# One block's shift in the attention heads' order, z kept in another buffer, and two clears on GpSimd

## The reference, cut to what matters

```python
y_a = hyena_mixer(hy, ...) @ P['w_hy_out'][l]
...
kv = (ckv @ P['w_kvb'][l]).reshape(B, L, N_HEADS, NOPE_DIM + V_DIM)
...
s = jnp.einsum('bqhd,bkhd->bhqk', qi, k).astype(jnp.float32) * scale
p = jax.nn.softmax(s, axis=-1).astype(v.dtype)
return jnp.einsum('bhqk,bkhd->bqhd', p, v)
...
y = (g_a * y_a + g_b * y_b + g_c * y_c) @ P['w_out'][l]
```

## Time and profile before

| | us |
|---|---|
| median of 3 runs | 3128.07 |
| lowest, highest | 3124.54, 3131.0 |
| profiled execution, its own time | 3132.21 |
| its span, first to last instruction | 3130.4 |

### The profile page before, as it was taken

The page is one execution under the profiler, slowest core; times in us unless marked ns, Lnnn a source line. Parts: engine busy times, 40 slices in busy tenths (PEclk is TensorE's granted clock), DMA queues, the critical chain, the costliest instruction groups (busy, mean ns, idle before and its releaser), DMA issues.

```text
span 3130.4 us, 48654 instructions
## 1 busy us (share of the span) xinstructions
PE 3014.3 (96%) x19892; PEld 2936.5 (94%) x19892; DVE 2124.1 (68%) x3521; ACT 1140.6 (36%) x1820; POOL 83.7 (3%) x160
## 2 busy tenths in 40 slices
PE   7999999999999999999999999999999999999998
PEld 4899999998899899999999999999888999999998
DVE  7677666646655557988967897863665555775675
ACT  3422312322444434434433433442244443443432
POOL 0000000000000000000000000000000000000000
PEclk8999999999999999999999999999999999999999
DMA  8255553245122432343332433324611252222222
GB/s 305 90 215 218 222 192 141 109 165 223 71 72 92 186 110 80 102 153 131 129 108 75 142 122 135 129 104 168 245 71 71 75 208 83 75 88 81 95 68 75
DMA packets 89743, 408.90 MB, mean 131 GB/s; under 512 B 10049, under 2 KB 13569, under 8 KB 68914
## 3 DMA queue, kind: packets, MB, share of 16 engines
q1 hardware_dynamic: 60960, 287.86, 25.5%
q0 software_dynamic: 19296, 92.43, 8.1%
q10 hardware_dynamic: 9266, 25.50, 2.2%
HBM read 359.46 MB, written 46.30 MB: 130 GB/s over the span
## 4 chain that ended last, share of the span: by engine, by line
PE 77%; DVE 14%; ACT 5%; issue 3%; DMA 1%; ACTq 0%; DVEq 0%
PE tile_psum L743 20%; PE misc_psum L860 12%; PE tile_psum L750 11%; PE misc_psum L864 6%; PE tile_psum L1215 6%; PE tile_psum L704 3%; PE tile_psum L1219 3%; PE misc_psum L669 3%; PE tile_psum L669 2%; PE tile_psum L860 2%; PE tile_psum L709 2%; PE misc_psum L1153 1%; DVE h L2254 1%; PE tile_psum L1080 1%; DVE wlo L2083 1%
## 5 line engine op out<-in xcount | busy, mean ns | idle before, releaser
L743 PE MATMUL tile_psum<-n_hi,whi 128*128 128x320 f32 x1536 | 353.4, 311 | 4.0 <-issue 2.2
L743 PE MATMUL tile_psum<-n_lo,whi 128*128 128x320 f32 x1536 | 351.2, 309 | 0.0
L2083 DVE TENSOR_TENSOR wlo<-raw,whi 128x2048 fp32r<-128x2048 f32 (+4 forms) x130 | 250.5, 1929 | 120.0 <-ACT whi L1491 118.0
L743 PE MATMUL tile_psum<-x_hi,whi 128*128 128x320 f32 x1300 | 298.9, 310 | 19.2 <-DVE h L2254 19.2
L743 PE MATMUL tile_psum<-x_lo,whi 128*128 128x320 f32 x1300 | 297.1, 309 | 0.0
L743 PEld LDWEIGHTS tile_psum<-n_hi,whi 128*128 128x128 f32 x1536 | 257.6, 189 | 6.8 <-DVE n_lo L2174 4.2
L743 PEld LDWEIGHTS tile_psum<-n_lo,whi 128*128 128x128 f32 x1536 | 258.3, 189 | 0.0
L1491 ACT ACTIVATE whi<-raw 128x2048 fp32r<-128x2048 f32 (+4 forms) x130 | 208.9, 1616 | 129.8 <-DMA raw<-in_w_down 42.1
L1215 PE MATMUL tile_psum<-n_hi,whi 128*128 128x320 f32 x768 | 237.6, 320 | 11.7 <-ACT gate_out L1978 10.3
L2254 DVE SCALAR_TENSOR_TENSOR h<-tile_psum,ada_t,h 128x320 f32<-128x320 f32 (+2 forms) x408 | 154.1, 434 | 129.6 <-PE tile_psum L750 128.1
L750 PE MATMUL tile_psum<-n_hi,wlo 128*128 128x320 f32 x1536 | 241.4, 309 | 0.0
(11 more groups left out here) (384 smaller groups left out, 6439.0 us busy)
## 6 DMA issues: line engine op xcount, KB each, us to landing
raw<-in_w_up SPq DMA_DIRECT2D x72, 512.0 KB, 3.9
raw<-in_w_up SPq DMA_DIRECT2D x34, 1024.0 KB, 4.8
w_ada<-in_w_ada POOLq DMA_DIRECT2D x68, 512.0 KB, 4.1
w_ada<-in_w_ada SPq DMA_DIRECT2D x60, 512.0 KB, 6.1
raw<-in_w_gate SPq DMA_DIRECT2D x24, 1024.0 KB, 4.8
raw<-in_w_down SPq DMA_DIRECT2D x29, 768.0 KB, 4.4
whi<-table_keep SPq DMA_DIRECT2D x20, 1024.0 KB, 4.7
wlo<-table_keep SPq DMA_DIRECT2D x20, 1024.0 KB, 6.9
```

Source lines behind the costliest of these rows:

```text
L743: pe.matmul(tps[:, t.s, m, 0:TH], blk(p, m * n + k)[0], (hi, lo)[b][:, k, tok], start=k == 0 and b == 0, stop=False)
L2083: ins = dve.tensor_tensor(lo_at(r, n)[:, 0:w], raw_at(r, n)[:, 0:w], hi_at(h_, n)[:, 0:w].bitcast(F32), ALU.subtract)
```

## The change: what it does

The order: in each pair the queries of the second head (Q, a gate half, QS) move from before the pair's first score block to before its second one. In the first pair z's split becomes a step of its own (Z), after N0 and before V0. The result is `Q0 F K0 QS0 F S0 F Q1 F QS1 S1 F N0 Z0 V0 S2` and, for the later pairs, `Q2 F K2 QS2 S10 F N9 T8 F Q3 F QS3 S11 F N10 T9 F P1`. The number of steps of each kind stays the same.

The last product of the Hyena branch is written to `art[:, c]` (the buffer of the scaled low-rank rows) in place of `hyx`, and ScalarE waits for both halves once, ahead of the first Q. The two clears leave VectorE; GpSimd makes them in its queue, ahead of the third gate write, after a wait for z.

```diff
--- before.py
+++ after.py
@@ -257,11 +257,13 @@
     for n in range(5 * HEADS + 2):
         if n < 5 * HEADS:
             if n % 10 == 0:
-                for hd in (n // 5, n // 5 + 1):
-                    order += [("Q", hd), ("F", 0)] + [("K", hd)] * (hd % 2 == 0) + [("QS", hd)] + [("F", 0)] * (hd == 0)
+                order += [("Q", n // 5), ("F", 0), ("K", n // 5), ("QS", n // 5)] + [("F", 0)] * (n == 0)
+            if n % 10 == 1 and n < 5 * HEADS:
+                order += [("Q", n // 5 + 1), ("F", 0), ("QS", n // 5 + 1)]
             order += [("S", n), ("F", 0)]
         if 1 <= n <= 5 * HEADS:
             order.append(("N", n - 1))
+            order += [("Z", 0)] * (n == 1)
         if n >= 2:
             order += [("T", n - 2)] + [("F", 0)] * (n != 2)
             if n % 5 == 1:
@@ -1444,6 +1446,10 @@
                             pool.wait_ge(g_kept[b], 16 * (12 * l + (3 * m + 4 - b) // 2))
 
                     for c in range(3 * KT):
+                        if c == 2:
+                            pool.wait_ge(z_new, 2 * (l + 1))
+                            pool.memset(kh1[ROPE:P - NOPE, :].bitcast(F32), 0.0)
+                            pool.memset(kl1[ROPE:P - NOPE, :].bitcast(F32), 0.0).then_inc(keys_cleared, 1)
                         if c == 3 * KT - 4:
                             pool.wait_ge(q_split, 1 + HEADS * (l + 1))
                             gates_kept(0)
@@ -1992,11 +1998,11 @@
                 def keep_z():
 
                     for c in range(2):
-                        act.wait_ge(z_new, due(z_new))
-                        split_hi(xh[:, c, :], hyx[:, 4 + c, :])
+                        split_hi(xh[:, c, :], art[:, c, :])
 
                 act.wait_ge(stored, due(stored, 16))
                 act.wait_ge(x_kept, due(x_kept, 32))
+                act.wait_ge(z_new, due(z_new, 2))
 
                 for what, n in HEAD_ORDER:
                     h_, qt = n // 5, n % 5
@@ -2006,9 +2012,9 @@
                         N, Q = NOPE_AT[n % 2], ROPE_AT[n % 2]
                         act.activation(halves(qf[N, :]), mps[N, t.s, :, 0:TH], ACT.Copy)
                         act.activation(qf[Q, TL:T], mps[Q, t.s, 1, TL - TH:TH], ACT.Copy).then_inc(q_copy, 1)
+                    elif what == "Z":
+                        keep_z()
                     elif what == "K":
-                        if n == 0:
-                            keep_z()
                         m = misc()
                         for k_, N in zip(khs, NOPE_AT):
                             split_hi(halves(k_[N, :]), mps[N, m.s, :, 0:KEYS // 2])
@@ -2800,7 +2806,7 @@
                     for c, t in enumerate(tiles):
                         v = hyx[:, 4 + c, :]
                         dve.wait_ge(t.free, t.free_at)
-                        dve.tensor_tensor(v, v, hyx[:, 2 * o + c, :], ALU.mult).then_inc(v_ready if o == 0 else z_new, 1)
+                        dve.tensor_tensor(art[:, c, :] if o else v, v, hyx[:, 2 * o + c, :], ALU.mult).then_inc(z_new if o else v_ready, 1)
                     if o == 0:
                         dve.wait_ge(v_ready, due(v_ready, 4))
 
@@ -2843,11 +2849,8 @@
                 def keep_z():
 
                     for c in range(2):
-                        lo_part(xl[:, c, :], hyx[:, 4 + c, :], xh[:, c, :], z_split)
-                    dve.wait_ge(z_split, due(z_split, 2))
-                    for k_ in (kh1, kl1):
-                        ins = dve.memset(k_[ROPE:P - NOPE, :].bitcast(F32), 0.0)
-                    ins.then_inc(keys_cleared, 1)
+                        lo_part(xl[:, c, :], art[:, c, :], xh[:, c, :], z_split)
+                    due(z_split, 2)
 
                 due(z_new, 2)
                 due(low_split, 4)
```

## The result

| | before | after |
|---|---|---|
| median, same chip | 3128.91 | 3156.11 |
| lowest, highest (4 runs each) | 3124.54, 3131.0 | 3153.45, 3158.91 |
| ratio, 95% interval | | 1.0089 [1.0074, 1.0104] |
| profiled execution, its span | 3130.4 | 3154.3 |

What follows compares the result with a forecast made beforehand. TensorE, busy 96% of the span and running in written order, was taken as the bound. Pair lateness 17.7 plus clock 10.8 minus start gain 3.0 gave +25.5 us on the median 3128.07: 3153.6 us, range 3139 to 3166.

Steps and rivals of the forecast that it cites:

- The chain and its cover: Later pairs: k_hi, k_lo, q_lo lose their 3.8 us cover; TensorE idles 3.95, 5.1, 3.95 us before first score blocks.
- What is late next: Later pairs: 14.91 us from first score block to P; P1, P3, P5 later by 3.2, 2.9, 2.7 us.
- The term of 8.8 us per layer: Summed lateness of P1, P3 and P5 in the later pairs, without clock; 17.7 us for two layers.
- Clock of the pairs: Low clock after the pairs' idle: 1.5 us four times, about 2.4 us twice, 10.8 us in all.
- Start: First pair: S0 waits 3.5 us, V0's wait goes; gain 0.7 to 2.2, taken as 1.5 us per layer.
- Costs put at nothing: ScalarE's z wait (0, at most 1.3 us) and GpSimd's wait and memsets (1 to 7 us each, covered): cost 0.
- The sum: Whole kernel, two layers: 17.7 + 10.8 - 3.0 = +25.5 us, giving 3153.6 us.
- One of the forecast's own signs of being wrong: Forecast would be wrong if the stage from Q0 to the last P weren't 10 to 15 us longer per layer.
- B: Rival: idle without clock cost, the clock holding or its low stretch hidden; 3140 to 3143 us, 13%.
- C: Rival: the new 1.7 us gap before P also drops the clock, six times; 3155 to 3164 us, 16%.
- E: Rival: no effect, an equal amount made up at later waits or order misread; 3122 to 3134 us, 5%.
- D: Rival: faster through earlier softmax of a pair's first block, if q_lo is ready when K2 ends; 3105 us, 4%.

Runs made afterwards that it cites:

- e5: Changed kernel with two gate halves of each later pair moved back ahead of its first score block: 3129.86 us, ratio 1.0005.
- e4: Changed kernel with 24, 30 and 24 unread matmuls added before the first score blocks of the three later pairs: 3149.78 us, ratio 1.0065.
- e10: Changed kernel with the query split (QS) of each pair's second head moved ahead of the pair's fourth score block: 3155.70 us, ratio 1.0103.
- e1: Kernel before with the new order alone, z and the clears left as they were: 3161.85 us, ratio 1.0104.
- e6: Changed kernel with the old order, but QS of each pair's second head moved behind P and V: 3118.05 us, ratio 0.9963.
- e2: Changed kernel with the old order of heads, keeping z's buffer, later split and GpSimd clears: 3124.28 us, ratio 0.9982.
- e3: Changed kernel with the new order in the first pair only, old order in the three others: 3126.02 us, ratio 0.9992.
- e7: Changed kernel, new order kept, with QS of each pair's second head moved behind P and V: 3155.39 us, ratio 1.0087.

## Why the prediction was right

*The chain and its cover.* Forecast 3.95, 5.1 and 3.95 us of idle, measured 3.87, 5.00 and 3.87, S10 where the old distances put it. e5 shows the cause: with cover the loss goes.

*What is late next.* The join of three (gate half, q_lo of head 3, S11's reduction) was forecast at 14.91 us from S to P and a wait of 1.7: e4 has 14.92, after 1.70. The gap of 1.31 before the gate half is gone, as said. The term of 8.8 us per layer is 8.9.

*Clock of the pairs.* This term was too small: 5.4 us per layer forecast, 6.7 measured. The second pair paid 1.56 (1.5 forecast) and the third 2.14 (2.4), but the fourth 2.97, because its low stretch was twice as long after the same idle. I had sized it by the length of the idle; these rows say that the idle's length doesn't set it. That the second pair hit its figure was luck: in the second layer of e10 the same idle of 3.87 us is followed by 3.4 us of lost clock at the second pair and by 1.7 at the fourth.

```profile
2355.00:2361.00 6.00, 5.67 (x22) 5.65 (x23) 1.57 (x5) 0.89 (x2) 0.00 (x0) 0.50 0.01 3
...
2505.00:2507.00 2.00, 2.00 (x9) 2.00 (x9) 0.86 (x2) 0.00 (x0) 0.00 (x0) 0.50 0.00 0
2507.00:2508.00 1.00, 1.00 (x6) 1.00 (x5) 0.47 (x3) 0.79 (x3) 0.00 (x0) 0.52 0.00 0
2508.00:2509.00 1.00, 1.00 (x9) 0.99 (x9) 0.00 (x0) 1.00 (x3) 0.00 (x0) 1.00 0.00 0
```

*Start.* Q1 and a gate half, put at 3.6 us, take 3.8 by the earlier trace rows (778.94 to 785.85, less the wait of 3.12), which changes nothing in the sum. S0, V0 and their waits came within 0.3 us of the forecast (3.73 idle for 3.5; V0 793.01 for 792.8), but the gain of 1.5 us per layer was 0.4: P0 is at 48.40 us from Q0 for 48.77. S2's wait of 0.93 us took back what V0's had given (S2 24.75 us from Q0 for 25.18), and a second low stretch came as before (796 to 800), where the forecast hoped for its absence.

*Costs put at nothing.* The trace before does hold compute instructions of GpSimd, four memsets of 128x1 at 0.1 us. The new memsets took 0.73 us each, less than the 1 to 7 forecast, and ended 15 us before ScalarE's head-1 copies. VectorE's operations beside them kept their durations (wlo 2.29 and q_rope_tmp 0.77 us, both as in before), so no shared path showed. ScalarE's wait for z showed as 1.5 us before Q0's copy, and this reached neither S0 nor the sum visibly.

*The sum.* By the stages it was 12.75 us per layer and is 15.1: the start gave 1.1 less than forecast, the clock cost 1.3 more. One of the forecast's own signs of being wrong, a stage not 10 to 15 us longer from Q0 to its last P, is thereby met by a hair: 15.1 us in each layer. P5 too is later than its sign said, by 5.6 us from its pair's first score block for 3 to 5. "I see no wait that would give this back" holds for the stages; outside them 6.3 us came back in the profiled execution, 5.0 of them lost clock. So two errors partly cancel in the total, and that 3156.1 lies within 3 us of 3153.6 is partly luck.

*The rivals.* B is out, since e4 gives the clock's share its own price. C is out at its place: no fall at any of the waits of 1.7 us before P, in after, e1 and e4, 18 in all; its level, 3155 to 3164, was met for another reason. It was near, since e5's 2.0 us at the same place were followed by a fall three times of six. E is out by the result. D is out as forecast: q_lo is 3.9 us late. e6 shows that its aim can be had, but not by this change.

## What to carry to other kernels

Before a step is moved in an in-order queue, ask what serial chain of the other engines it covers, not only whether its own inputs are ready; what looks like a queue with 0.17 us of idle may hide 3.9. Where a later consumer is delayed by work on other engines, move that work alone (here the split) and leave the matmuls where they cover. Look at what else moves with a step, too: where other steps are placed by counting, they shift. When an idle place is added to a busy matmul stream, price it twice, as idle and as low clock behind it, and compare stages, saying how much of a difference is lost clock, since low stretches elsewhere move the total by some us.

## What the runs showed of the hardware

- The low stretches of TensorE's clock (1.2 for 2.4 GHz) lose 1.7 us, or 3.4, or in a row 5.1, at full use of the engine. What is lost isn't a property of the place or of the idle before it: 3.87 us of idle was followed by 1.7 in the second pair and 3.4 in the fourth in after, and the other way round in the second layer of e10; 2.99 us before V0 in e2 by 5.1 in one layer and 1.7 in the other. What decides it stays open.
- Idle alone doesn't decide: after the 0.93 us before S2, behind 18 matmuls of 128 columns (V0), the clock fell in both layers, as at the eight such places of e1, e3, e4 and e5, while 1.70 us before P, behind matmuls of 320 columns, left it at 1.00 six times, and 2.20 us before T0 in e7 twice. The windows of after at the first place:

```profile
795.00:796.00 1.00, 0.13 (x2) 0.00 (x0) 0.65 (x3) 0.88 (x3) 0.00 (x0) 1.00 0.00 0
796.00:797.00 1.00, 0.94 (x5) 0.94 (x6) 0.01 (x1) 1.00 (x4) 0.37 (x1) 0.73 0.79 139
797.00:800.00 3.00, 3.00 (x13) 3.00 (x13) 3.00 (x4) 1.28 (x2) 0.17 (x1) 0.52 0.93 378
```

  The TensorE: Matmul & The Clock Gate page of the Trainium skill (section "HAM oscillation — how this bites in real kernels") speaks of bursts shorter than the waits between them; this place, a short wait after a busy stretch, isn't of that kind and fell too. Nor are the six pair starts, behind each of which TensorE works for 14.8 us or more before it waits again: that sentence alone doesn't reach the places to which the forecast applied it, though the clock did fall at all six.
- Matmuls whose result nobody reads kept the clock at 1.00 through 4 us of waiting (e4), for a gain of 1.56 to 2.97 us per place, but they have to fit the wait: where they ran over, they cost time.
